# Experts in blocks of 64 rows, gathered as half rows and multiplied in two column tiles; S5 Toeplitz matrices in 32-column tiles

## The reference, cut to what matters

```python
# S5: a state space of 64 complex states per group of 16 channels, 16 groups
_, _, xr, xi = lax.associative_scan(_complex_affine_combine, (a_r, a_i, bu_r, bu_i), axis=1)
y = einsum('gcp,blgp->blgc', C_re, xr) - einsum('gcp,blgp->blgc', C_im, xi)

# experts: each token goes to the best of 4 groups, and to the best 2 of its 8 experts (32 in all)
expert = gsel[:, None] * EXPERTS_PER_GROUP + top_i          # 2048 x 2 pairs of token and expert
h = silu(xb @ w_gate[e]) * (xb @ w_up[e])                   # 1024 -> 512, twice
y = h @ w_down[e]                                           # 512 -> 1024
out[token] += gate * y
```

## Time and profile before

| | us |
|---|---|
| median of 3 runs (2447.6 to 2457.45) | 2454.18 |
| the profiled execution, whole | 2454.5 |
| its span | 2452.7 |
| TensorE matmul busy | 2269.7 (93%) |
| VectorE busy | 1406.5 (57%) |
| ScalarE busy | 986.8 (40%) |
| GpSimd busy | 366.0 (15%) |

### The profile page before, as it was taken

The page is one execution under the profiler, slowest core; times in us unless marked ns, Lnnn a source line. Parts: engine busy times, 40 slices in busy tenths (PEclk is TensorE's granted clock), DMA queues, the critical chain, the costliest instruction groups (busy, mean ns, idle before and its releaser), DMA issues. The chain is left out here.

```text
span 2452.7 us, 34881 instructions
## 1 busy us (share of the span) xinstructions
PE 2269.7 (93%) x11993; PEld 1292.3 (53%) x11994; DVE 1406.5 (57%) x2047; ACT 986.8 (40%) x1418; POOL 366.0 (15%) x275
## 2 busy tenths in 40 slices
PE   7999999999979998999999999399999999999990
PEld 3565565655668974555555555144544545445440
DVE  7566555665569753333333332777557677777753
ACT  5432433323221342222222221256446576666653
POOL 0021121210220000000000000012222223222222
PEclk9999999999989998999999999599999999999995
DMA  7001001002051152111111100579677899998957
GB/s 249 39 27 61 1 27 61 1 27 46 9 214 35 44 188 96 36 69 44 61 69 51 45 35 35 181 260 313 212 241 271 292 316 320 333 307 300 318 179 289
DMA packets 155062, 349.50 MB, mean 142 GB/s; under 512 B 28496, under 2 KB 39120, under 8 KB 154704
## 3 DMA queue, kind: packets, MB, share of 16 engines
q1 hardware_dynamic: 140128, 310.32, 34.8%
q0 software_dynamic: 13680, 33.58, 5.8%
q10 hardware_dynamic: 1152, 4.19, 0.4%
HBM read 303.48 MB, written 60.82 MB: 149 GB/s over the span
## 5 line engine op out<-in xcount | busy, mean ns | idle before, releaser
L111 PE MATMUL bankA<-main_room,hnT 128*128 128x512 f16 (+1 forms) x1536 | 302.2, 355 | 4.1 <-DVE main_room L639 4.1
L111 PE MATMUL bankE<-wg,xT 128*128 128x512 f16 x1128 | 254.3, 382 | 5.9 <-DVE xT L2542 5.6
L111 PE MATMUL bankE<-wd,hT 128*128 128x512 f16 x1128 | 251.2, 379 | 2.6 <-DVE hT L2547 2.6
L111 PE MATMUL bankE<-wu,xT 128*128 128x512 f16 x1128 | 251.1, 379 | 0.0
L111 PEld LDWEIGHTS bankA<-main_room,hnT 128*128 128x128 f16 x1536 | 150.8, 99 | 146.9 <-issue 9.0
L111 PEld LDWEIGHTS bankE<-wg,xT 128*128 128x128 f16 x1128 | 110.9, 99 | 141.9 <-issue 11.9
L111 PE MATMUL bankA<-hnT,main_room 128*128 128x512 f16 x768 | 172.5, 387 | 8.9 <-issue 6.8
L111 PEld LDWEIGHTS bankE<-wd,hT 128*128 128x128 f16 x1128 | 109.9, 98 | 126.3 <-issue 3.5
L111 PEld LDWEIGHTS bankE<-wu,xT 128*128 128x128 f16 x1128 | 110.4, 98 | 122.7
L111 PE MATMUL bankC<-w_out_s,catT 128*128 128x512 f16 x768 | 171.3, 384 | 2.5 <-DVE w_probs L1914 2.5
L2519 DVE SCALAR_TENSOR_TENSOR wg<-w_rows,wg 128x2048 f16<-128x2048 f32 x64 | 143.7, 2287 | 49.9 <-ACT wg L2294 49.9
(11 more groups left out here) (389 smaller groups left out, 3276.7 us busy)
## 6 DMA issues: line engine op xcount, KB each, us to landing
w_rows<-in_w_gate SPq DMA_DIRECT2D x64, 1024.0 KB, 8.5
w_rows<-in_w_up SPq DMA_DIRECT2D x64, 1024.0 KB, 8.1
w_rows<-in_w_down SPq DMA_DIRECT2D x64, 1024.0 KB, 10.3
cat_t<-scratch_cat SPq DMA_DIRECT2D x16, 512.0 KB, 4.8
main_room<-in_x SPq DMA_DIRECT2D x16, 512.0 KB, 5.5
scratch_ybuf<-main_room SPq DMA_DIRECT2D x16, 512.0 KB, 2.6
out<-hf SPq DMA_DIRECT2D x16, 512.0 KB, 11.0
x_room<-in_x SPq DMA_DIRECT2D x3, 2048.0 KB, 10.8
```

Source lines behind the costliest of these rows:

```text
L111: ins = pe.matmul(o, a[x][k], b[y][k], start=start and k == 0 and j == 0, stop=stop and k == n - 1 and j == 2)
```

## The change

S5: the eight products of a group go into four column tiles of 32 columns each, two into each tile. Experts: blocks hold 64 rows of one expert. A gathered row is half a token: partitions 0 to 63 hold the first halves of the 64 tokens, 64 to 127 the second halves, and `rows` is one list for gather and add. Gate and up lie side by side in `wgu`; each product takes 64 columns of tokens and 512 columns of weights, and a pair of them writes partitions 0 to 63 and 64 to 127 of one bank. `xr`, `xT`, `sg`, `hT`, `y` and their banks become pairs. The adds still wait for each other. Splits of gate and up stand together in the first block's step, those of down in the step after. The tables `in_block`, `rows`, `gate_of` and the plan grow from 64 to 98 columns; `in_block` now lies in slot 1 of `wgu`, so this slot is first filled after the gates are listed. Cut to its core ("..." where lines are left out):

```diff
-                    for s in range(SBL):
-                        a = (SBL - 1 - s) * S5C
-                        ins = pe.matmul(bank[3][:, gg * P:(gg + 1) * P], BZ[:, gg, a:a + LK], CZ[:, q % 2, gg, a:a + LK],
-                                        start=(s == 0), stop=(s == SBL - 1))
+                    for late in range(2):
+                        b = (SBL - 1 - late) * S5C
+                        for j in range(SBL // 2):
+                            a = (SBL - 1 - 2 * j - late) * S5C
+                            r = slice(2 * j * S5C, 2 * (j + 1) * S5C)
+                            ins = pe.matmul(bank[3][r, gg * P:(gg + 1) * P], BZ[:, gg, b:b + 2 * S5C], CZ[:, q % 2, gg, a:a + LK],
+                                            start=(late == 0), stop=(late == 1), skip_group_check=True)
...
+HB = P // 2
+NB = 2 * T // HB + NE
+MIN_TURNS = USED_MIN // 2 - 2
+NBT = NB + 2
...
+            from_rows, to_rows = (t.rearrange("t (h n) -> (t h) n", h=2) for t in (dram["xn_scr"], dram["ybuf"]))
             def gather(b):
-                if b:
-                    pool.wait_ge(xt, 2 * b)
...
+                if b >= 2:
+                    pool.wait_ge(xt, b - 1)
+                pool.indirect_dma_start(xr[:, b % 2, :], None, from_rows, bass.IndirectOffsetOnAxis(ap=rows[:, b:b + 1], axis=0),
+                                        bounds_check=2 * T - 1, oob_is_err=False).then_inc(x_ld[b % 2], 16)
+            def add(b):
                 if b:
                     pool.wait_ge(y_st, b * 16)
-                pool.wait_ge(y_t, b * 2 + 2)
...
+                pool.wait_ge(y_t, b + 1)
+                pool.indirect_dma_start(to_rows, bass.IndirectOffsetOnAxis(ap=rows[:, b:b + 1], axis=0), y[b % 2], None,
+                                        bounds_check=2 * T - 1, oob_is_err=False, compute_op=ALU.add).then_inc(y_st, 16)
...
+                    for b in (2 * r, 2 * r + 1):
+                        gather(b + 4)
+                        if b >= 2:
+                            add(b - 2)
...
 (ScalarE)
-            def step(b):
-                take_h(b - 1)
-                silu(b)
-                following(act, b, gates(b))
-                take_x(b + 1)
-                following(act, b, ups_downs(b))
-                take_y(b - 1)
+            def step(b, p):
+                silu(b, p)
+                take_h(b - 1, 1 - p)
+                take_x(b + 2, p)
+                following(act, b, gate_up_split(b))
+                take_y(b - 2, p)
+                following(act, b - 1, down_split(b - 1))
...
 (VectorE)
+            def first():
...
+                product(0, 0)
+                x_rest(2, 0)
+                gate_up_rest(1, 1)
+                product(1, 1)
+                h_rest(0, 0)
+                x_rest(3, 1)
...
+            def step(b, p):
+                product(b, p)
+                h_rest(b - 1, 1 - p)
+                x_rest(b + 2, p)
+                following(dve, b, gate_up_rest)
+                following(dve, b - 1, down_rest)
...
 (TensorE)
+            def in_halves(o, tokens, rows, ks, n):
+                for k in ks:
+                    for j, (x, z) in enumerate(((0, 0), (0, 1), (1, 0))):
+                        for half in range(2):
+                            ins = pe.matmul(o(half), tokens(x, k), rows(z, k, half), start=k == 0 and j == 0, stop=k == n - 1 and j == 2, skip_group_check=True)
...
+            def step(b, p):
+                by_slot(b, gate_up(b, p))
+                turn_h(b - 1, 1 - p)
+                turn_x(b + 2, p)
+                by_slot(b - 2, down(b - 2, p))
```

More of the change, by code:

```diff
@@ L2175, in place, with among_first @@
         def place(p, slot, part):
-            _, w, k, a = pieces[p]
-            return w[:, slot, part, k:k + a, :]
+            _, g, k, a = pieces[p]
+            return wd[:, slot, part, k:k + a, :] if g is None else wgu[:, slot, part, k:k + a, g, :]
+        def among_first(b, n):
+            return isinstance(b, int) and b < n
         def following(eng, b, split):
@@ L2269, in steps @@
+            for p in range(2):
+                pool.wait_ge(x_ld[p], used * 16 + 48)
+            pool.wait_ge(y_st, used * 32 + 64)
         def steps(eng, first, step, last):
             first()
-            eng.wait_ge(planned, 1)
+            for b in (2, 3):
+                step(b, b % 2)
             used = turns_used(eng)
@@ L2323, in take_h @@
-            def take_h(b):
-                act.wait_ge(ht, b + 1)
[L2325 to L2329, removed]
-                    act.wait_ge(yd, b * 2 + j + 1)
-                    act.activation(y[:, j * 512:(j + 1) * 512], bank[5 + j][:, :], ACT.Copy, scale=1.0 / (W_SCALE * H_SCALE)).then_inc(taken, 1)
+                    act.wait_ge(yd, b)
@@ L2648, in gate_up, with down, o, tokens @@
                 return products_of
-            def down(b, more=True):
+            def down(b, p):
                 def products_of(slot, u):
-                    pe.wait_ge(lo_dn, u * 2 + 2)
+                    def o(half):
+                        return YB[p][half * HB:(half + 1) * HB, :]
+                    def tokens(x, n):
+                        return hT[p][:, x, n % 2 * 2 + n // 2, :]
+                    def rows_of(z, n, half):
+                        return wd[:, slot, z, n, half * W:(half + 1) * W]
@@ L2653, in products_of @@
                     pe.wait_ge(h_hi, b + 1)
                     pe.wait_ge(h_lo, b + 1)
-                    if more:
-                        pe.wait_ge(y_t, b * 2)
-                    for j in range(2):
-                        products(pe, bank[5 + j][:, :], [[hT[:, h, n, :] for n in range(FT)] for h in range(2)],
-                                 [[wd[:, slot, h, n, j * 512:(j + 1) * 512] for n in range(FT)] for h in range(2)]).then_inc(yd, 1)
-                return products_of
-            def step(b):
-                by_slot(b, gate_up(b, lambda: turn_h(b - 1)))
-                turn_x(b + 1)
-                by_slot(b - 1, down(b - 1))
+                    if not among_first(b, 2):
+                        pe.wait_ge(y_t, b - 1)
@@ L2680, in _, with last @@
+            def last(n):
+                turn_h(n - 1, 1)
+                by_slot(n - 2, down(n - 2, 0))
+                by_slot(n - 1, down(n - 1, 1))
             steps(pe, first, step, last)
```

338 lines of the change are left out of this document (171 added, 167 removed).

## The result

| | before | after |
|---|---|---|
| median, us (runs) | 2451.7 (4) | 2374.3 (4: 2373.7 to 2378.9) |
| ratio, 95% interval | | 0.9682, 0.9665 to 0.9698 |
| profiled execution, span, us | 2454.5, 2452.7 | 2374.1, 2371.9 |
| S5's outputs done (L1601, now L1604, starts), us | 881.4 | 869.3 |
| first add starts, last add lands, us | 1630.1, 2402.7 | 1615.2, 2324.1 |

A forecast was written before the change was run, and what follows sets the result against it. The prediction took the chain of adds, one at a time, to bound the changed experts: 768 us, 6 us less at their end. With S5's -12: 2454.5 - 6 - 12 = 2436 us, range 2356 to 2500.

The forecast's parts named there:

- The block: Experts: a 64-row block takes TensorE 8.68 us, with paired column-tile products overlapping, 80 blocks 694 us.
- rival on the tiles: Two rivals in experts: weight loads show in tiles, 2667 us, chance 0.04; paired tiles don't overlap, 2977 us, chance 0.02.
- S5: Toeplitz products in four tiles save 2.3 us in each of three rounds and 5.2 in the last: -12 us together.
- VectorE's first wait: Sign in S5: VectorE's first wait for TensorE in a round (1.74 us) goes, the second (3.28) becomes about 1 us.
- The transfers: Experts: weights and rows need 620 to 686 us, half rows maybe tens more, hidden; as the bound: 2430 us, chance 0.07.
- hidden under 768: 768 us is the forecast length of the experts' chain of 80 adds, one after another, against 773 before.
- The price of an add among loads: Experts: an add while weights load costs 11.0 us, 10.2 to landing plus 0.8 to the next; ends 9.5 and 12.5.
- The split of 60 loaded and 20 quiet adds: Experts: 662 us of load time holds 60 of the 80 adds; the other 20 run in quiet and take 106 us.
- the quiet price: Experts: an add with no loads beside it costs 5.3 us, 4.5 to landing plus 0.8 to the next.
- TensorE stays the bound: Rival in experts: loaded adds nearer 8.5 us or fewer, so TensorE's blocks set the time; -87, with S5 2356 us; chance 0.20.
- the tail: The time behind the last add's landing, after the experts: claimed untouched.

The follow-up runs named there:

- 12 and 12: The changed kernel with 12 products of one column tile, then 12 of the other, instead of alternating pairs: 2670.9 us in one run.
- Groups of 3: The changed kernel with three products in the upper column tile, then three in the lower, and so on: 2385.6 us in one run.

## Why the prediction was wrong in size

**The block** (8.68 us): right, 8.69, so neither rival on the tiles holds: the two of a pair run together, and their weight loads of 110 ns are hidden.

**S5** (-12): about right, -11. A round shrank by the 2.3 us worked out. VectorE's first wait went, but its second is not 1 us:

```profile
803.39 1.22 DVE L1416 TENSOR_TENSOR main_room<-TC,vbank 128x1024 f32<-128x1024 f32 x1 [2.83 <-PE vbank L1563]
...
854.35 1.22 DVE L1416 TENSOR_TENSOR main_room<-TC,vbank 128x1024 f32<-128x1024 f32 x1 [3.60 <-PE vbank L1563]
```

In the first of these rounds it is 2.83 us. Both waits of before were 1.74 + 3.28 = 5.02 us, and 5.02 - 2.28 = 2.74: the 1.74 us that vanished were part of the same 2.3, and I had taken both away. In the two rounds after that it is 4.26 and 3.60 us, and there TensorE's granted clock was lower:

```profile
799.63 3.72 PE L1563 MATMUL vbank<-main_room,BmT 128*128 128x256 f32 x16 [0.36 <-ACT BmT L1505]
...
824.02 5.14 PE L1563 MATMUL vbank<-main_room,BmT 128*128 128x256 f32 x16 [0.36 <-ACT BmT L1505]
...
824.00:829.00 5.00, 4.98 (x16) 4.00 (x16) 0.91 (x3) 1.88 (x3) 0.00 (x0) 0.71 0.31 105
```

The last line is the stretch of the second one; its clock is 0.71 of full speed, 2.4 GHz in a part of it and 1.2 GHz in the rest. TensorE had stood for 2.75 us just before, in its new wait for VectorE's L1437. In S5 of the kernel before, it waited for 0.3 us a round at most from the second round on, and the clock was 1.00 from 740 to 910. Each of the 11 other traces with the new loop also has such a stretch in S5. So I estimate that the lower clock takes back (4.26 - 2.83) + (3.60 - 2.83) = 2.2 us of what the loop gives. By the profile the stage gained 108.0 - 98.5 = 9.5 us. The other 2.5 of the 12.1 us in the table lie ahead of the stage, where nothing was changed.

**The transfers** (hidden under 768): hidden under 709 too, at a share of 0.93.

**The price of an add among loads**: this step failed. "Among loads I take 10.2 + 0.8 = 11.0, between 9.9 for few rows and 11.7 for many." The 80 adds, sorted by the rate of the loads from the end of POOL's part to the landing (times are means in us):

| loads beside it | adds | start to landing | of it, to land |
|---|---|---|---|
| under 50 GB/s | 18 | 4.74 | 3.11 |
| 200 to 300 GB/s | 39 | 8.90 | 6.23 |
| over 300 GB/s | 23 | 7.63 | 5.82 |

The split of 60 loaded and 20 quiet adds was right (62 and 18), and so was the quiet price with 0.8 us to the next (forecast 5.3, measured 4.74 + 0.79 = 5.53). Among loads the mean is (39 x 8.90 + 23 x 7.63) / 62 = 8.43, with the 0.79 9.22 us instead of 11.0: 62 x 9.22 + 18 x 5.53 = 671 us instead of 768. The reason lies in the row I leaned on. The add with 6 rows and 9.9 us started while a split ran, in the kernel before:

```profile
1718.43 3.68 POOL L2242 DMA_INDIRECT scratch_ybuf<-y,rows_to  x1 [7.53 <-ACT y L2331]
...
1716.17 4.48 DVE L2519 SCALAR_TENSOR_TENSOR wd<-w_rows,wd 128x2048 f16<-128x2048 f32 x2
```

The split ended at 1716.17 + 4.48 = 1720.65, so POOL's part took 3.68 us and only 6.2 of the 9.9 us were the transfer. I took the wait for a split as part of what every add pays beside loads; 32 of the 80 pay it, 1.5 us each. Among loads the mean 8.43 is 2.35 of POOL's part and 6.08 of transfer, so of the 1.8 us between 10.2 and 8.43 POOL's part makes 1.3 and the transfer the rest. The trace of before had the rule in all 30 adds that start in a split.

**TensorE stays the bound** was the right rival, with the condition it named (adds "nearer 8.5 us"). Its 686 us from first add to last landing became 709, because of 25 us of late pairs, nearly all at the turns of the loop. This is a second term that the prediction had at nothing: I had priced the sequencer's work at zero, since before it is covered, and had not asked what halving the time of the queued products does to that cover. That rival's experts were to give 87 us and gave 67; the other few us between 25 and 20 are the tail (50.0 to 47.8 us) and differences between executions.

## What to carry to other kernels

A time from issue to landing is a sum. Read the engine's own part of a sample apart from its transfer before using it as a price, above all when the sample is one row. Making queued work denser also shortens what it covers, so look at the sequencer's branches and loads at every turn of a loop. A stage that got shorter can leave TensorE standing, so look at the granted clock there too. And after a loop body is made longer, look whether the packets of the instruction queue grow.

## What the runs showed of the hardware

- Products of two column tiles need not be neighbours to overlap: with 12 and 12 a product for a free tile starts ahead of about four waiting ones that are earlier in the program. Groups of 3 cost 8.70 us a block as pairs do, 12 and 12 cost 12.30. The Trainium skill ("TensorE: Matmul & The Clock Gate", What overlaps and what doesn't) says products start in strict order; the lines at 1903.08 and 1903.29 speak against it. What the Trainium skill has in "TensorEngine Tiling (Array Packing)", Key Properties, that different tiles run weight loads and products in parallel, agrees with 8.69 us a block.
- A loop of TensorE with six blocks of code (1800 weight loads and products) fetched about 9 packets of 16 KB anew in each of its 8 long turns, and TensorE stood for 9 to 15 us each time; with four blocks of code it fetched nothing anew.
- After TensorE had stood for 2.75 us in S5, the granted clock fell from 2.4 to 1.2 GHz in two of the rounds; in one of them 16 records of L1563 took 5.14 us instead of 3.72. One more stand of 2.76 us was not followed by this.
- When POOL issued an indirect DMA while a split of VectorE ran, its part took the rest of the split plus 1.46 us, instead of 1.59 (30 of 30 before, 32 of 33 after).
